# Two attention steps scored together on VectorE, and their softmax sums finished in shared one-by-two instructions

## What is computed

```
first block
  A: p = softmax(q1 k1) - lam * softmax(q2 k2), 4 heads, query blocks of 128, keys up to the block's end
  B: softmax(q k + bias), 8 heads, same query blocks
  C: softmax(q mem_k) over 256 memory rows, 4 heads
second block
  N (16 heads, groups of four share keys), gates g0, g1, g2:
     out = g0 * softmax_c(31 compressed keys) v_c + g1 * softmax_s(causal) v_s + g2 * softmax_w(window of 512) v_w
  X: softmax(q mem_k) over 256 memory rows, 4 heads
```

## Time and profile before

| | us |
|---|---|
| median of 3 runs (lowest, highest) | 2438.45 (2434.14, 2439.51) |
| the profiled execution's own time | 2438.51 |
| its span | 2436.5 |
| PE busy in the span | 2291.6 (94%) |
| DVE busy | 1216.2 (50%) |
| ACT busy | 976.5 (40%) |
| GpSimd busy | 145.4 (6%) |

### The profile page before, as it was taken

One profiled execution on the slowest core, in us unless ns is written; L12 is line 12 of the kernel. 1 busy time (PEld: TensorE's weight loads), 2 busy tenths in 40 slices (PEclk: granted clock), 3 DMA queues, 4 the chain that ended last, 5 costly groups with the idle time before them and its releaser, 6 DMA issues.

```text
span 2436.5 us, 29732 instructions
## 1 busy us (share of the span) xinstructions
PE 2291.6 (94%) x10984; PEld 1814.7 (74%) x10984; DVE 1216.2 (50%) x2216; ACT 976.5 (40%) x1618; POOL 145.4 (6%) x120
## 2 busy tenths in 40 slices
PE   5899999988898999999999989989899999999997
PEld 4788888866666777888888777767455688888886
DVE  4433335674455546434444647662889655432432
ACT  5432223454456333333223422623778534322321
POOL 1000001201010000100001420000000001000011
PEclk9999999988999999999999999999899999999998
DMA  4323322321201223322322272122000132333331
GB/s 182 115 87 94 112 87 77 122 69 35 78 27 35 95 86 111 96 89 86 119 86 82 91 234 73 67 71 88 18 2 1 48 109 88 102 98 92 99 91 51
DMA packets 213468, 206.76 MB, mean 85 GB/s; under 512 B 4832, under 2 KB 194400, under 8 KB 213120
## 3 DMA queue, kind: packets, MB, share of 16 engines
q1 hardware_dynamic: 210368, 192.31, 25.1%
q0 software_dynamic: 3008, 13.24, 1.7%
HBM read 199.25 MB, written 4.19 MB: 83 GB/s over the span
## 4 chain that ended last, share of the span: by engine, by line
PE 81%; DVE 10%; ACT 4%; issue 3%; DMA 2%; POOL 0%; SPq 0%; ACTq 0%; DVEq 0%; POOLq 0%
PE ps L870 24%; PE ps L871 24%; PE ps L872 24%; DVE Sm L825 2%; DVE wlo L615 2%; PE ps L721 2%; ACT whi L608 2%; PE ps L733 2%; DMA wraw<-in_w_in 1%; PE ps L1045 1%; PE ps L1037 1%; DVE st L847 1%; PE ps L1085 1%; DMA xin<-in_x 1%; PE ps L1110 1%
## 5 line engine op out<-in xcount | busy, mean ns | idle before, releaser
L615 DVE TENSOR_TENSOR wlo<-wraw,whi 128x2048 fp32r<-128x2048 f32 x192 | 440.4, 2294 | 424.0 <-ACT whi L608 424.0
L870 PE MATMUL ps<-hH,whi 128*128 128x512 f32 x1528 | 600.9, 393 | 19.1 <-DVE wlo L615 15.0
L871 PE MATMUL ps<-hL,whi 128*128 128x512 f32 x1528 | 596.5, 390 | 0.0
L872 PE MATMUL ps<-hH,wlo 128*128 128x512 f32 x1528 | 596.4, 390 | 0.0
L608 ACT ACTIVATE whi<-wraw 128x2048 fp32r<-128x2048 f32 x192 | 366.9, 1911 | 471.5 <-PE ps L872 440.9
L870 PEld LDWEIGHTS ps<-hH,whi 128*128 128x128 f32 x1528 | 287.5, 188 | 89.1 <-DVE wlo L615 21.7
L872 PEld LDWEIGHTS ps<-hH,wlo 128*128 128x128 f32 x1528 | 287.4, 188 | 61.0
L871 PEld LDWEIGHTS ps<-hL,whi 128*128 128x128 f32 x1528 | 287.7, 188 | 60.7 <-issue 1.0
L870 PE MATMUL ps<-gH,whi 128*128 128x512 f32 x608 | 236.5, 389 | 0.0
L871 PE MATMUL ps<-gL,whi 128*128 128x512 f32 x608 | 236.5, 389 | 0.0
L872 PE MATMUL ps<-gH,wlo 128*128 128x512 f32 x608 | 236.5, 389 | 0.0
(11 more groups left out here) (334 smaller groups left out, 2657.7 us busy)
## 6 DMA issues: line engine op xcount, KB each, us to landing
wraw<-in_w_in SPq DMA_DIRECT2D x45, 1024.0 KB, 5.0
wraw<-in_ffn_wg SPq DMA_DIRECT2D x22, 1024.0 KB, 5.1
wraw<-in_ffn_wu SPq DMA_DIRECT2D x22, 1024.0 KB, 5.1
wraw<-in_w_up SPq DMA_DIRECT2D x16, 1024.0 KB, 5.3
wraw<-in_w_down SPq DMA_DIRECT2D x16, 1024.0 KB, 5.3
wraw<-in_ffn_wd SPq DMA_DIRECT2D x16, 768.0 KB, 4.6
wraw<-in_w_gate SPq DMA_DIRECT2D x12, 1024.0 KB, 4.9
wraw<-in_ffn_wd SPq DMA_DIRECT2D x16, 640.0 KB, 4.4
```

The costliest lines, as they stand in the source:

```text
L615: dve.tensor_tensor(wlo[s][:, :], wraw[s][:, :], f32(whi[s][:, :]), ALU.subtract).then_inc(w_lo[s], 1)
L870: pe.matmul(o, lh, rh, start=start, stop=False)
L871: pe.matmul(o, lh, rl, start=False, stop=False)
L872: return pe.matmul(o, ll, rh, start=False, stop=stop)
```

## The change

DVE's list in the attentions is written by pairs. For each pair it now scores both steps, then normalises both steps of the pair before. In `normalise` one reciprocal, and for w one correction, work on two neighbouring columns of `st`. For the w steps of the last query block the two small instructions after the scores are shared by the pair too. ACT does the small exp of the correction for two columns at once, at the even slot of a w pair, and waits for both steps' `s_masked` before it. PE's list, the lag, the banks, the tiles Sm and the copies of ACT stay as they were.

```
--- before.py
+++ after.py
@@ -762,10 +762,11 @@
                     if e.m == "c":
                         act.activation(e.Sm[:, 0:e.n], e.Sm[:, 0:e.n], ACT.Exp).then_inc(s_exp, 1)
                     else:
-                        if e.m == "w":
-
+                        if e.m == "w" and slot % 2 == 0:
+
+                            act.wait_ge(s_masked, e.s + 2)
                             at = (52 if e.qt == TT - 1 else 8) + e.c
-                            act.activation(st[:, 48 + e.c:49 + e.c], st[:, at:at + 1], ACT.Exp)
+                            act.activation(st[:, 48 + e.c:50 + e.c], st[:, at:at + 2], ACT.Exp)
                         act.activation(e.Sm[:, 0:e.n], e.Sm[:, 0:e.n], ACT.Exp, bias=st[:, 8 + e.c:9 + e.c],
                                        scale=-1.0, accum_out=st[:, 12 + e.c:13 + e.c]).then_inc(s_exp, 1)
                 t = slot - (lag - 1)
@@ -804,59 +805,67 @@
         def dve_attention(dve, order, names, mask_of, gate_of=None):
             seq, lag = steps(names)
             last = len(seq) - 1
-            for slot in range(len(seq) + 1):
-                if slot <= last:
-                    e = seq[slot]
-                    s_, n = e.Sm, e.n
-
-                    dve.wait_ge(s_full, e.s + 1)
-                    if e.m == "c":
-                        order(dve.tensor_tensor(s_[:, 0:n], e.bank[:, 0:n], C("mask_cmp"), ALU.add))
-                        v = s_[:, 0:n].rearrange("p (q k) -> p q k", q=TT)
-                        order(dve.tensor_reduce(st[:, 32:36], v, AX.X, ALU.max))
-                        dve.tensor_tensor(v, v, st[:, 32:36].unsqueeze(2).broadcast_to([P, TT, NC32]), ALU.subtract).then_inc(s_masked, 1)
-                    else:
-                        if e.kind == "B" and e.qt == 0:
-
-                            dve.wait_ge(bias_ready, e.i * 2 + e.h + 1)
-
-                        dve.sem_inc(s_taken, 1)
-                        neg_max = st[:, 8 + e.c:9 + e.c]
-                        scored = dve.tensor_tensor_reduce(s_[:, 0:n], e.bank[:, 0:n], mask_of(e, n), -1.0,
-                                                          0.0 if e.m == "w" and e.qt < TT - 1 else 3e38, ALU.add, ALU.min, neg_max)
-                        if e.m == "w" and e.qt == TT - 1:
-
-                            order(scored)
-                            order(dve.tensor_scalar(st[:, 52 + e.c:53 + e.c], neg_max, 0.0, None, ALU.min))
-                            scored = dve.tensor_tensor(neg_max, neg_max, C("pad_cap")[:, e.qt:e.qt + 1], ALU.min)
-                        scored.then_inc(s_masked, 1)
-                if slot:
-                    e = seq[slot - 1]
-                    s_, n, c = e.Sm, e.n, e.c
-                    dve.wait_ge(s_exp, e.s + 1)
-                    if e.m == "c":
-                        v = s_[:, 0:n].rearrange("p (q k) -> p q k", q=TT)
+            def score(e):
+                s_, n = e.Sm, e.n
+
+                dve.wait_ge(s_full, e.s + 1)
+                if e.m == "c":
+                    order(dve.tensor_tensor(s_[:, 0:n], e.bank[:, 0:n], C("mask_cmp"), ALU.add))
+                    v = s_[:, 0:n].rearrange("p (q k) -> p q k", q=TT)
+                    order(dve.tensor_reduce(st[:, 32:36], v, AX.X, ALU.max))
+                    dve.tensor_tensor(v, v, st[:, 32:36].unsqueeze(2).broadcast_to([P, TT, NC32]), ALU.subtract).then_inc(s_masked, 1)
+                    return
+                if e.kind == "B" and e.qt == 0:
+
+                    dve.wait_ge(bias_ready, e.i * 2 + e.h + 1)
+
+                dve.sem_inc(s_taken, 1)
+                scored = dve.tensor_tensor_reduce(s_[:, 0:n], e.bank[:, 0:n], mask_of(e, n), -1.0,
+                                                  0.0 if e.m == "w" and e.qt < TT - 1 else 3e38, ALU.add, ALU.min,
+                                                  st[:, 8 + e.c:9 + e.c])
+                if e.m == "w" and e.qt == TT - 1:
+                    order(scored)
+                else:
+                    scored.then_inc(s_masked, 1)
+
+            def normalise(a, b):
+                c = a.c
+                dve.wait_ge(s_exp, b.s + 1)
+                if a.m == "c":
+                    for e in (a, b):
+                        v = e.Sm[:, 0:e.n].rearrange("p (q k) -> p q k", q=TT)
                         order(dve.tensor_reduce(st[:, 36:40], v, AX.X, ALU.add))
                         order(dve.reciprocal(st[:, 40:44], st[:, 36:40]))
                         order(dve.tensor_tensor(st[:, 44:48], st[:, 40:44], gate_of(e), ALU.mult))
                         dve.tensor_tensor(v, v, st[:, 44:48].unsqueeze(2).broadcast_to([P, TT, NC32]), ALU.mult).then_inc(s_norm, 1)
+                    return
+                if a.m == "w":
+                    order(dve.scalar_tensor_tensor(st[:, 12 + c:14 + c], st[:, 48 + c:50 + c], C("pads")[:, a.qt:a.qt + 1],
+                                                   st[:, 12 + c:14 + c], ALU.mult, ALU.add))
+                order(dve.reciprocal(st[:, 16 + c:18 + c], st[:, 12 + c:14 + c]))
+                if a.kind == "A":
+
+                    order(dve.tensor_tensor(st[:, 17 + c:18 + c], st[:, 17 + c:18 + c], gs[:, 3:4], ALU.mult))
+                for e in (a, b):
+                    s_, n, r = e.Sm, e.n, st[:, 16 + e.c:17 + e.c]
+                    if e.kind == "A" and e.m == 1:
+                        dve.wait_ge(s_norm, a.s + 1)
+                        dve.scalar_tensor_tensor(s_[:, 0:n], s_[:, 0:n], r, a.Sm[:, 0:n], ALU.mult, ALU.add).then_inc(s_norm, 1)
+                    elif e.kind == "N":
+                        dve.tensor_scalar(s_[:, 0:n], s_[:, 0:n], r, gate_of(e), ALU.mult, ALU.mult).then_inc(s_norm, 1)
                     else:
-                        if e.m == "w":
-                            order(dve.scalar_tensor_tensor(st[:, 12 + c:13 + c], st[:, 48 + c:49 + c], C("pads")[:, e.qt:e.qt + 1],
-                                                           st[:, 12 + c:13 + c], ALU.mult, ALU.add))
-                        order(dve.reciprocal(st[:, 16 + c:17 + c], st[:, 12 + c:13 + c]))
-                        if e.kind == "A" and e.m == 1:
-
-                            order(dve.tensor_tensor(st[:, 16 + c:17 + c], st[:, 16 + c:17 + c], gs[:, 3:4], ALU.mult))
-                            dve.scalar_tensor_tensor(s_[:, 0:n], s_[:, 0:n], st[:, 16 + c:17 + c], seq[slot - 2].Sm[:, 0:n],
-                                                     ALU.mult, ALU.add).then_inc(s_norm, 1)
-                        elif e.kind == "N":
-                            dve.tensor_scalar(s_[:, 0:n], s_[:, 0:n], st[:, 16 + c:17 + c], gate_of(e),
-                                              ALU.mult, ALU.mult).then_inc(s_norm, 1)
-                        else:
-                            dve.tensor_scalar(s_[:, 0:n], s_[:, 0:n], st[:, 16 + c:17 + c], None, ALU.mult).then_inc(s_norm, 1)
-                            if e.kind == "A":
-                                dve.wait_ge(s_norm, e.s + 1)
+                        dve.tensor_scalar(s_[:, 0:n], s_[:, 0:n], r, None, ALU.mult).then_inc(s_norm, 1)
+
+            for slot in range(0, len(seq) + 2, 2):
+                for e in seq[slot:slot + 2]:
+                    score(e)
+                if slot <= last and seq[slot].m == "w" and seq[slot].qt == TT - 1:
+                    c = seq[slot].c
+                    order(dve.tensor_scalar(st[:, 52 + c:54 + c], st[:, 8 + c:10 + c], 0.0, None, ALU.min))
+                    dve.tensor_tensor(st[:, 8 + c:10 + c], st[:, 8 + c:10 + c], C("pad_cap")[:, TT - 1:TT].broadcast_to([P, 2]),
+                                      ALU.min).then_inc(s_masked, 2)
+                if slot:
+                    normalise(seq[slot - 2], seq[slot - 1])
 
         def attention_over(eng, name):
```

## The result

The changed kernel takes **2574.3 us** (median of 4 runs, 2571.9 to 2576.4) against 2438.8 beside it: a ratio of 1.056, interval 1.054 to 1.058, or +136 us. The prediction said 2537 with a range up to 2575. The time is at the very end of that range, 37 us above the number. The profiled execution took 2571.9 us, its span is 2570.1.

A forecast was written before the change was run, and what follows sets the result against it. It took PE and DVE, overlapping in the attentions, to become a ring after the change: +83.3 us for the handoffs and +15.2 for clock spells on 2438.5 gave 2537 us, range 2508 to 2575 (chance 0.80).

The forecast's parts named there:

- the ring: In the attentions' pairs, PE's next scores wait for slot-2's normalisation, now behind two scores; engines take turns: +83.3 us.
- Its length in N: N's pairs at 3.28 us for s, 3.62 for w, 4.6 for c: 255.0 against 190.7, +64.3 us.
- the clock's term: One spell of lower TensorE clock at the start of each of N's four maps, 3.8 us each: +15.2 us.
- Rival 1: N, B and C spend half the time at the lower clock: 55 us more, 2577 us; chance 0.07 (beyond 2575).
- The sign that I named for it: In N, turns of three blocks last twice their 0.55 us for long stretches, with pairs as reckoned: Rival 1.
- B: In stage B, 14 pairs take 40.7 us for 36.0, plus 1.5 at the end: +6.2 us.
- C: In stage C, six pairs take 15.9 us for 11.8; a head's values and 1.0 at the end add: +6.4 us.
- X: In stage X, pairs take 20.4 us against 17.8, plus 0.8 for the first pair and 1.0 at the end: +4.4.
- A: In stage A, PE's longest wait gets another normalisation, 0.7 us in each of four heads: +2 us.
- An instruction of two columns: On DVE, a two-column reciprocal costs the same as one column, 0.20 us; a quarter more would save 6 us less.
- Rival 2: In the attentions, DVE is the bound and the saved instructions' 33.3 us come off: 2405 us; chance 0.03.
- Rival 3: The ring is partly slack, PE and DVE overlap more and the clock stays: +20 to +65, about 2485; chance 0.09.

The follow-up runs named there:

- e1: The changed kernel with TensorE's lag raised from three to four slots in N and X: 2452.3 us, ratio 1.0067.
- e5: The changed kernel with DVE's list interleaved (score, shared reciprocal, gate slot-2, score, gate slot-1), lag 3, small exp and clamp per step: 2500.6 us.
- e8: The changed kernel with TensorE's repeated transposes as in e4, and once more in w pairs of four blocks: 2547.9 us, ratio 1.0451.
- the second trace of before: The kernel before, unchanged, profiled once more: 2433.8 us.
- e4: The changed kernel with TensorE repeating the odd step's transposes once or twice while it waits, in B, N and X: 2547.7 us, ratio 1.0458.
- e12: The kernel before with the changed form (pairs, shared reciprocal) in A only: 2435.0 us, ratio 1.0001.
- e6: The interleaved order of e5 with a lag of four in N and X: 2432.3 us, ratio 0.9977.
- e9: e6 with B and C scored and normalised step by step as in the kernel before: 2426.2 us, ratio 0.9964.

## Why the prediction was right about the ring and wrong about the clock

- **The ring**: right. e1 opens it by the lag alone and N goes back to 190.3; e5 takes one score off it, and its full-clock s pairs of two to four blocks and w pairs of three are shorter by about that score (0.3 to 0.6 us).
- **Its length in N** (255 us): 265 measured. Per pair 3.28 was 3.39 for s, 3.62 was 3.78 for w, 4.6 was 4.83 for c (265 is an estimate, see e8). +10 us.
- **The step that failed is the clock's term**: "I take a spell in each of four maps: +15.2" was 40 us in N. It took the price of a spell from a map in which TensorE was busy for 95% (47.9 of 50.2 us), and that price was right there (the second trace of before has the map without the spell, 3.9 us shorter). The number of spells was wrong: 15 and not four. After the change TensorE is idle for 77 us of N (305.6 less 228.5; before 190.7 less 176.3, 14 us), about a microsecond in a pair, and the clock falls again and again, in w pairs of three and four blocks and some s pairs as well as in c pairs. By e4 and e8 more work for TensorE keeps the clock up and makes N shorter. That c pairs leave TensorE most idle was wrong too: in the last three maps it is idle for at most 1.8 us in one, and for 1.3 to 2.8 in a w pair of four blocks. The Trainium skill's section on idle gaps between bursts ("TensorE: Matmul & The Clock Gate", section "HAM oscillation — how this bites in real kernels") tells of a kernel whose TensorE waits for DMA between bursts and finds the lower clock after each wait. Here the waits are for VectorE, none longer than 2.8 us but for the one at N's start, and the clock fell as well: the direction agrees, and the size had to come from these runs.
- **Rival 1** (the clock decides more, 55 us over N, B and C by its sum) is what happened in N and B, 40 and some 6 us, and not in C, whose clock stayed at 1.00. It was given too little; its 2577 is nearer to the result than my number, and that the time still lies inside my range is luck: the range's high end had been put nearly at rival 1. The sign that I named for it came as well, in part: turns of three blocks last 0.90 us for 0.55 in the low stretches. Its argument against itself, that TensorE has more to do per pair than in A, was read from the kernel before, where TensorE hardly waits.
- **B** (+6.2, was +13.6): the ring's periods were right (3.25 us for three blocks at the full clock, reckoned 3.27). With its full-clock means all 14 pairs would take 43 us (40.7 reckoned); they took 49. The 6 between are the clock again, 0.84 in B (0.91 before), for which the sum had no term.
- **C** (+6.4, was +3.3): its six pairs take 15.8 us, 15.9 reckoned; the 1.3 that I added for a head's values isn't there on top of them, nor the 1.0 at the end (from the last pair to N it is 953.6 us in both traces), and the first pair is 0.7 shorter than before (0.88 for 1.57).
- **X** (+4.4) was +5.4. **A** (+2) was -3.7 in this trace and nothing that the timing of e12 shows: one more normalisation ahead of TensorE's longest wait cost nothing that can be seen. Why is not shown.
- **An instruction of two columns** costs what one of one column does: right (0.16 us for either reciprocal).
- **Rival 2**, DVE is the bound and 33 us come off: out. With the ring open (e1) N takes 190.3 us, what it took before; with DVE interleaved as well (e6, e9) 9.7 us of N come off against the first trace of before and 5.8 against the second, while DVE's work there is some 17 us less. **Rival 3**, slack in the ring: out, the rounds add up without any.

The misses add up: N's ring +10, N's clock +25, B +7, X +1, C -3, A -6: +34 of the 35 between +98.5 reckoned and +133.6 in the spans.

## What to carry to other kernels

Before instructions are grouped for fewer fixed costs, look up in the other engine's list which result it wants next: if the grouped order makes that result wait for inputs that the other engine sends only after it, two overlapping engines become a ring, and the saving is the small number. The lag between producer and consumer has to grow with the group (here from 3 to 4 for groups of two), and the wanted result belongs straight behind the shared part, ahead of the second score. When a change will make TensorE wait in every period, price the lower clock for a large part of the stretch, and not by the few spells seen while it was busy.

## What the runs showed that I had not expected

- More matmuls made the stretch shorter: 227 repeated transposes in N, 21.7 us less, clock 0.88 for 0.76.
- Two instructions on different tiles back to back start closer together than their length: two gates of 128x384 take 0.87 us together, of 128x256 0.73, where one takes 0.48 and 0.41.
- The kernel before showed two lengths of N, 3.9 us apart by one clock spell, in two executions of the same program. A profile of each is needed before a difference of 4 us between two traces is given to an edit.
